# Prompt scores of the latent heads from multiplied-out keys: one product of 96 rows per score block in place of two

## What is computed

```python
kv = (c_kv @ w_ukv).reshape(B, T, A_HEADS, A_NOPE + A_VDIM)
k_nope, v = kv[..., :A_NOPE], kv[..., A_NOPE:]
s = (einsum('bqhd,bkhd->bhqk', qn, k_nope)          # prompt, 64 numbers per head
     + einsum('bqhr,bkr->bhqk', qr, k_r)) * scale   # 32 rotary numbers
...
q_lat = einsum('bqhd,chd->bqhc', q_nope, w_uk)      # samples: the query goes into the latent space
s_past = (einsum('bqhc,bkc->bhqk', q_lat, past_c)
          + einsum('bqhr,bkr->bhqk', q_rope, past_r)) * scale
```

## Time and profile before

| what | value |
|---|---|
| median of 3 runs | 2074.73 us (2072.35 to 2075.08) |
| the profiled execution | span 2076.9 us from its first to its last instruction; no other time of it is on record |
| PE busy | 2055.7 us, 99% of the span |
| DVE, ACT, POOL busy | 1530.8, 1284.6, 119.9 us |
| latent score steps of layer 0 / layer 1 | from 91.7 us / from 1121.2 us of the span |

### The profile page before, as it was taken

The page is one execution under the profiler, slowest core; times in us unless marked ns, Lnnn a source line. Parts: engine busy times, 40 slices in busy tenths (PEclk is TensorE's granted clock), DMA queues, the critical chain, the costliest instruction groups (busy, mean ns, idle before and its releaser), DMA issues.

```text
span 2076.9 us, 40622 instructions
## 1 busy us (share of the span) xinstructions
PE 2055.7 (99%) x15546; PEld 1794.8 (86%) x15546; DVE 1530.8 (74%) x3491; ACT 1284.6 (62%) x2535; POOL 119.9 (6%) x138
## 2 busy tenths in 40 slices
PE   8999999999999999999999999999999999999998
PEld 6776799999999888788887758999999998887887
DVE  5844589868899776576678436998688997766766
ACT  5464445658888665565564544556688886555654
POOL 2200010000000010100022000100000001101000
PEclk9999999999999999999999999999999999999999
DMA  9443437776666888898763543577766668888886
GB/s 313 154 150 143 163 126 254 248 253 221 216 215 214 286 304 296 303 319 279 253 226 141 170 170 116 180 253 250 246 221 209 220 214 300 311 290 295 266 269 220
DMA packets 137376, 481.76 MB, mean 232 GB/s; under 512 B 25666, under 2 KB 42082, under 8 KB 130768
## 3 DMA queue, kind: packets, MB, share of 16 engines
q1 hardware_dynamic: 124640, 438.45, 62.6%
q0 software_dynamic: 10496, 40.42, 5.6%
q10 hardware_dynamic: 2048, 0.30, 0.1%
HBM read 475.83 MB, written 104.21 MB: 279 GB/s over the span
## 4 chain that ended last, share of the span: by engine, by line
PE 98%; DVE 1%; ACT 1%; DMA 0%; issue 0%; DVEq 0%; ACTq 0%
PE ps L1194 35%; PE ps L1241 33%; PE ps L827 4%; PE ps L875 4%; PE ps L919 3%; PE ps L1206 3%; PE ps L1157 2%; PE ps L927 2%; PE ps L1165 1%; PE ps L1161 1%; PE ps L884 1%; PE ps L1016 1%; PE ps L1180 1%; PE ps L1019 1%; PE ps L978 1%; PE ps L1032 1%
## 5 line engine op out<-in xcount | busy, mean ns | idle before, releaser
L2165 DVE TENSOR_TENSOR parts<-region,parts 128x1024 fp32r<-128x1024 f32 x512 | 625.6, 1222 | 300.6 <-ACT parts L1509 298.0
L1194 PE MATMUL ps<-tokens_hi,parts 128*128 128x256 f32 x4096 | 760.5, 284 | 0.0
L1509 ACT CAST parts<-region 128x1024 fp32r<-128x1024 f32 x512 | 538.8, 1052 | 271.0 <-PE ps L1241 221.2
L1241 PE MATMUL ps<-parts,parts_hw 128*128 128x512 f32 x3024 | 688.7, 389 | 0.0
L1241 PEld LDWEIGHTS ps<-parts,parts_hw 128*128 128x128 f32 x3024 | 566.8, 188 | 124.0 <-DVE parts_hw L2215 6.9
L1194 PEld LDWEIGHTS ps<-tokens_hi,parts 128*128 128x128 f32 x4096 | 636.6, 188 | 1.0 <-issue 0.8
L1194 PE MATMUL ps<-parts_hw,parts 128*128 128x256 f32 x2048 | 573.7, 280 | 0.0
L1194 PEld LDWEIGHTS ps<-parts_hw,parts 128*128 128x128 f32 x2048 | 386.5, 189 | 0.0
L1555 ACT ACTIVATE big<-ps 128x256 f32<-128x256 f32 (+31 forms) x252 | 131.7, 523 | 146.9 <-PE ps L1194 146.8
L1543 ACT CAST parts_hw<-big 128x256 fp32r<-128x256 f32 x256 | 170.9, 668 | 0.7 <-DVE big L2226 0.7
L1536 ACT ACTIVATE region<-region 128x128 f16<-128x128 f16 x512 | 169.2, 436 | 0.0
(11 more groups left out here) (316 smaller groups left out, 2172.9 us busy)
## 6 DMA issues: line engine op xcount, KB each, us to landing
region<-in_peer_uT SPq DMA_DIRECT2D x256, 512.0 KB, 4.1
region<-in_peer_v SPq DMA_DIRECT2D x256, 512.0 KB, 4.7
out<-in_state_win_k SPq DMA_DIRECT2D x112, 384.0 KB
out<-in_state_win_v SPq DMA_DIRECT2D x112, 384.0 KB
big<-in_window_keysT SPq DMA_DIRECT2D x16, 576.0 KB, 3.8
big<-in_state_win_v SPq DMA_DIRECT2D x48, 192.0 KB, 4.2
region<-in_w_out SPq DMA_DIRECT2D x4, 2048.0 KB, 8.2
big<-in_peer_wq SPq DMA_DIRECT2D x4, 2048.0 KB, 13.7
```

Source lines behind the costliest of these rows:

```text
L1194: mm = pe.matmul(ps[:, j % ZB, 0:SEQ], a, hp[b][:, c, :], start=(c == 0 and n == 0), stop=(c == KD - 1 and n == 2))
L1241: mm = pe.matmul(ps[:, 2 * half + t, :], w_t[a][:, 128 * t:128 * t + 128], v_t[b][:, 512 * half:512 * half + 512], start=(j == 0 and n == ...
L1509: act.copy(hi_t[n % HIGHS], rows_t[n % ROWS]).then_inc(high[l], 1)
L2165: dve.tensor_tensor(lo_t[n % ROWS], rows_t[n % ROWS], hi_t[n % HIGHS], ALU.subtract).then_inc(low[l], 1)
```

## The change

The keys of the prompt are multiplied out once per layer. Three new products `kn` (`wuk` by the latents, two heads each, 256 columns) give the 64 key numbers of each head; DVE copies them to `khT`, rows 0 to 63, one head per copy, and before that writes the rotary keys of all six heads to rows 64 to 95 with one copy (32 partitions by 1536). The queries `qhT` are transposed head by head, 96 rows (64 and the rotary 32) at once, six jobs in place of the five of `qnT` and `qrT`. The score job is then one matmul per block, over 96 rows. The product into the latent space is left for the 8 sample tokens alone (`ql`, six matmuls of 8 columns into one bank). `kn` and `va` move ahead of `qbT` and `kbT`. `wuk` is a new load of 192 KB; `ukT` is laid out with 64 rows of 3072 bytes in place of 128 of 1536. ACT copies each half of `q` at once.

```diff
 jobs += [(("q", t, n), "A") for t in range(3) for n in range(2)]
+jobs += [(("kn", g), "V") for g in range(HP)]
+jobs += [(("va", t), "A") for t in range(2)]
 jobs += [(("qbT", g), "V") ...] + [(("kbT", g), "V") ...]
-jobs += [(("qnT", g), "A") for g in range(HP)] + [(("qrT", g), "A") for g in range(2)] + [(("qrS",), "A")]
-jobs += [(("qlT", h), "V") for h in range(NH)]
-jobs += [(("va", t), "A") for t in range(2)]
+jobs += [(("qhT", h), "A") for h in range(NH)] + [(("qrS",), "A")]
+jobs += [(("ql",), "V")]
...
 # SP
-sp.dma_start(wuv..., wukv_src[:, 1]).then_inc(uq_ld, 16)
+for a, dst in enumerate((wuk, wuv)):
+    sp.dma_start(dst..., wukv_src[:, a]).then_inc(uq_ld, 16)
...
 # PE
+wait_moved(pe, "ckvT")
+for g in range(HP):
+    dense(("kn", g), [(wuk[:, 128 * g:128 * g + 128], ckvT[:, 0:SEQ])], 128, SEQ)
+for t in range(2):
+    dense(("va", t), [(ckvT[:, 128 * t:128 * t + 128], wuv)], 128, 384)
...
-for g in range(HP):
-    turn("qnT", g, parts=tokens(q, 128 * g))
 pe.wait_ge(q_ready, 1)
-for g, hs in enumerate((4, 2)):
-    turn("qrT", g, parts=tokens(q, NH * NOPE + 128 * g, 32 * hs))
+for h in range(NH):
+    turn("qhT", h, parts=tokens(q, UQ // NH * h, NOPE + ROPE))
 turn("qrS", ...)
-wait_moved(pe, "qnT", HP - 1)
+wait_moved(pe, "qhT", NH - 1)
+o = begin("ql")
 for h in range(NH):
-    dense(("qlT", h), [(ukT[r0:r0 + 64, h // 2, :], qnT[r0:r0 + 64, h // 2, :])], 128, T)
-for t in range(2):
-    dense(("va", t), ...)
-wait_moved(pe, "qlT", NH - 1)
+    mm = pe.matmul(o[:, NB * h:NB * h + NB], ukT[:, h, :], qhT[0:NOPE, h, SEQ:T], start=True, stop=True)
+mm.then_inc(product[now[0]], 1)
+wait_moved(pe, "kn", HP - 1)
...
-pe.matmul(o[:, c0:c0 + K], qlT[:, h, qs], ckvT[:, 0:K], start=True, stop=False)
-mm = pe.matmul(o[:, c0:c0 + K], qrT[r0:r0 + 32, h // 4, qs], krT[r0:r0 + 32, 0:K], start=False, stop=True)
+mm = pe.matmul(o[:, c0:c0 + K], qhT[:, h, qs], khT[:, h, 0:K], start=True, stop=True)
...
 # DVE, behind the copy that announces q_ready
+wait_moved(dve, "krT")
+step(dve.tensor_copy(khT[NOPE:NOPE + ROPE], krT[NOPE:NOPE + ROPE, 0:SEQ].unsqueeze(1).to_broadcast([ROPE, NH, SEQ])))
+for g in range(HP):          # head_keys(g)
+    o = read("kn", g)
+    step(dve.tensor_copy(khT[0:NOPE, 2 * g, :], o[0:NOPE, 0:SEQ]))
+    settle()
+    dve.tensor_copy(khT[0:NOPE, 2 * g + 1, :], o[NOPE:128, 0:SEQ]).then_inc(moved_v[now[0]], 1)
 # qbT and kbT copies, taps
-for h in range(NH):
-    o = read("qlT", h)
-    dve.tensor_copy(qlT[:, h, :], o[:, 0:T]).then_inc(moved_v[now[0]], 1)
 step(dve.memset(qlS, 0.0))
-dve.tensor_copy(qlS[:, :, 0:NH], qlT[:, :, SEQ:T]...).then_inc(spread_set, 1)
+o = read("ql")
+dve.tensor_copy(qlS[:, :, 0:NH], o[:, 0:48]...).then_inc(moved_v[now[0]], 1)
```

More of the change, by code:

```diff
@@ L275, in program @@
         W_AT = at[0]
[L276 to L279, removed]
+        dead = big[:, at[0]:at[0] + NB * LAT]
+        ukT = cut(NH * LAT)[0:NOPE].rearrange("p (h c) -> p h c", h=NH)
+        qhT = cut(NH * T)[0:NOPE + ROPE].rearrange("p (h t) -> p h t", h=NH)
+        khT = cut(NH * SEQ)[0:NOPE + ROPE].rearrange("p (h t) -> p h t", h=NH)
         qkT = cut(2 * HP * T)
@@ L1394, in _ @@
                         o = read("q", t, n)
-                        oh = o[0:m, 0:288].rearrange("p (h x) -> p h x", h=3)
-                        qn = q[0:m, t, 192 * n:192 * n + 192].rearrange("p (h x) -> p h x", h=3)
-                        qr = q[0:m, t, NH * NOPE + 96 * n:NH * NOPE + 96 * n + 96].rearrange("p (h x) -> p h x", h=3)
-                        act.copy(qn, oh[:, :, 0:NOPE])
-                        act.copy(qr, oh[:, :, NOPE:]).then_inc(moved_a[now[0]], 1)
-                for g in range(HP):
-                    o = read("qnT", g)
-                    act.copy(qnT[:, g, :], o[:, 0:T]).then_inc(moved_a[now[0]], 1)
-                o = read("qrT", 0)
-                act.copy(qrT[:, 0, :], o[:, 0:T]).then_inc(moved_a[now[0]], 1)
-                o = read("qrT", 1)
-                act.copy(qrT[0:64, 1, :], o[0:64, 0:T]).then_inc(moved_a[now[0]], 1)
+                        act.copy(q[0:m, t, 288 * n:288 * n + 288], o[0:m, 0:288]).then_inc(moved_a[now[0]], 1)
+                for t in range(2):
+                    o = read("va", t)
+                    act.copy(va[:, t, :], o[:, 0:384]).then_inc(moved_a[now[0]], 1)
+                for h in range(NH):
+                    o = read("qhT", h)
+                    act.copy(qhT[:, h, :], o[0:NOPE + ROPE, 0:T]).then_inc(moved_a[now[0]], 1)
                 o = read("qrS")
@@ L1410, in _ @@
                 e.then_inc(moved_a[now[0]], 1)
-                for t in range(2):
-                    o = read("va", t)
-                    act.copy(va[:, t, :], o[:, 0:384]).then_inc(moved_a[now[0]], 1)
                 for s in range(2 * NH + 2):
@@ L1803, in _ @@
                 settle()
-                dve.tensor_copy(qrr[0:NB], q[0:NB, 2, NH * NOPE:].rearrange("p (h c) -> p h c", h=NH).unsqueeze(2).to_broadcast([NB, NH, 4, ROPE])).then_inc(q_ready, 1)
+                dve.tensor_copy(qrr[0:NB], q[0:NB, 2, :].rearrange("p (h c) -> p h c", h=NH)[:, :, NOPE:].unsqueeze(2).to_broadcast([NB, NH, 4, ROPE])).then_inc(q_ready, 1)
+                wait_moved(dve, "krT")
+                step(dve.tensor_copy(khT[NOPE:NOPE + ROPE], krT[NOPE:NOPE + ROPE, 0:SEQ].unsqueeze(1).to_broadcast([ROPE, NH, SEQ])))
+                for g in range(HP):
+                    head_keys(g)
                 for g in range(HP):
@@ L1811, in _ @@
                 some_taps(TAPS_AHEAD[4])
-                for h in range(NH):
-                    o = read("qlT", h)
-                    dve.tensor_copy(qlT[:, h, :], o[:, 0:T]).then_inc(moved_v[now[0]], 1)
-                settle()
-                dve.wait_ge(moved_v[now[0]], READ["qlT", NH - 1][1])
                 dve.wait_ge(product[now[0]], NUM["qrS",] + 1)
@@ L1819, in _ @@
                 settle()
-                dve.tensor_copy(qlS[:, :, 0:NH], qlT[:, :, SEQ:T].rearrange("p h b -> p b h")).then_inc(spread_set, 1)
+                o = read("ql")
+                dve.tensor_copy(qlS[:, :, 0:NH], o[:, 0:48].rearrange("p (h b) -> p b h", h=NH)).then_inc(moved_v[now[0]], 1)
                 def past_max(b):
```

27 lines of the change are left out of this document (11 added, 16 removed).

## The result

| | before | after |
|---|---|---|
| median | 2072.15 us (2066.55 to 2075.08, 8 runs) | 2078.93 us (2074.85 to 2082.25, 8 runs) |
| ratio, 95% interval | | 1.0031 [1.0019, 1.0043] |
| span of the profiled execution | 2076.9 us | 2080.4 us |
| PE at 0.50 in it, without the last 6 us | 17.1 us | 44.4 us |

A forecast was written before the change was run, and what follows sets the result against it. PE, busy 99% of the span, was the bound. Per layer: scores -7.7, added work +1.8, waits +0.4, given back +2.4, sum -3.1 us; -6.2 for two layers from 2074.7 gave 2068.5 us, range 2064.0 to 2073.0.

The forecast's parts named there:

- Query products, `kn` and `va`: PE ahead of the scores: `kn` adds 1.4 us per layer; `va`, priced at 1.36 us, only moves.
- 42 transpositions: PE ahead of the scores: 42 transpositions in place of 39, +0.5 us per layer.
- `ql`: Product for the sample tokens ahead of the scores: 1.5 us against `qlT`'s 1.57, so nothing gained or lost.
- Score job: Latent head's scores on PE: 0.76 us instead of 2.09, saving 7.7 us per layer for six heads.
- Given back: Score steps 1 to 4: PE held back by ACT loses 1.2, 1.2, 0.8 and 0.1 us again, rounded sum 2.4 per layer.
- A pair of copies of `kn`: DVE's copies, 0.73 us per pair, hold the banks of `kbT`; PE waits some 0.2 to 0.3 us.
- the `ukT` layout: Load of `ukT` in another layout with the same bytes: costed at nothing; PE had waited 0.46 us for it.
- even or equal: Rule that DVE copies within SBUF run at double speed if both sides' outermost dimensions are so; wide copy priced 0.9 us.
- rivals 1 and 2: Scores stay at 1.05 us per head, 2069.6 us, chance 0.12; DVE's wide copy runs slow, 2070.1 us, chance 0.12.
- rival 5: TensorE's clock falls ahead of the score steps, 12 us low per layer, making the kernel slower: 2080.5 us; chance 0.06.
- The one row against the fall, 85 to 90 at 1.00: Argument against the clock falling: from 85 to 90 us, nearly all transpositions and half-array work, it stayed 1.00.
- PHASE: Rival in the experiments' expectations, not the prediction: clock falls come and go whatever the order of work; no chance given.

The follow-up runs named there:

- e3: Changed kernel with DVE's wide copy of the rotary keys moved ahead of the rotation of q, PE's order untouched; 2070.46 us, ratio 1.0.
- the second execution of before: The kernel before, unchanged, profiled once more; 2066.74 us, span 2064.9.
- e9: Kernel before with its latent product cut to 8 columns per head, `va` kept in place and no wait added; 2073.4 us, ratio 1.0001.
- e7: Kernel before with seven small DVE copies ahead of the copies of `qbT` and `kbT`, so PE waits among its transpositions; 2079.41 us, ratio 1.0031.
- e10: Changed kernel with wide copy ahead of q's rotation, `ukT` awaited only ahead of `ql`, `kn` and `va` spread at three places between transpositions; 2066.7 us, ratio 0.9977.
- e4: Changed kernel with `ukT`'s load on its own semaphore, awaited ahead of `ql` instead of the query products; 2078.68 us, ratio 1.0034.
- e5: Changed kernel with `kn` and `va` behind `kbT`, wide copy behind the copies of `kbT`, `ukT` awaited only ahead of `ql`; 2071.6 us, ratio 0.9993.
- e8: Changed kernel plus sixteen unread filler matmuls of 256 columns, two passes each, ahead of `ql`; 2091.05 us.
- e2: Changed kernel with `kn` and `va` moved behind `kbT`, DVE's wide and head copies behind its `qbT` and `kbT` copies; 2073.01 us, ratio 1.0011.
- e6: Changed kernel with wide copy ahead of q's rotation, `kn` and `va` together behind `kbT`, `ukT` awaited only ahead of `ql`; 2069.04 us, ratio 0.9991.
- e1: Changed kernel plus one dense filler matmul of 256 columns ahead of each of the nine `kbT` and `qhT` jobs per layer; 2081.44 us.

## Why the prediction was wrong

**The sum was right, for full clock.** It said nothing of how long the clock would hold. Its parts by the rows of e3, layer 0:
- Query products, `kn` and `va`: 8.80 for 34 passes against 6.12 for 24, +2.7; forecast 1.4 + 1.36. 42 transpositions: 6.65, +0.6; forecast +0.5. `ql` 1.43; forecast 1.5.
- Score job: 0.76 at 92.50 and 0.66 at 95.45. In the changed kernel, at full clock: 0.66, 0.83, 0.69, 0.85, 0.76 for heads 1 to 5; mean 0.76, as forecast.
- Given back, by the distance that the 20 transpositions of a step take, 2.24 before (93.83 to 96.07): 2.69 in step 1 of e3 (96.11 to 98.80), 3.28 in step 2 of the changed kernel (108.34 to 111.62) and 0.2 more at `SC` 1, 3.12 in step 3 (116.24 to 119.36). So 0.45, 1.25 and 0.9, forecast 0.3, 1.2 and 0.8 (the changed kernel itself has 0.3 in step 1). The idle times in the brackets are smaller (0.34, 0.67 + 0.16, 0.47): part of the holding back is in the pace.
- The block: 55.53 against 59.00, -3.5. The forecast, without the waits that e3 takes out, was -7.7 + 1.8 + 2.4 = -3.5.

**Two small terms were short.** A pair of copies of `kn` comes each 0.90 us (85.24 to 86.14), not 0.73: so 0.63 us of waits in place of 0.2 to 0.3 (the prediction's own times of banks and jobs add up to 0.4). And the `ukT` layout, costed at nothing, was not nothing: PE waited 1.20 and 1.09 us in place of 0.46 and 0.42. From issue to landing the load took 3.1 and 3.0 us, against 2.3 in the second execution of before, and in both traces the DMA engines had nothing to do for over 2 us ahead of it, so `wuk`'s load wasn't in its way. That it is the smaller number of longer rows I read from these traces alone; the load wasn't tried in the old layout.

**Two readings were loose, and nothing hangs on them.** L1748 goes over 3 token groups on both sides, so by the prediction's words "even or equal" it would be fast too, yet its 384 elements took the 0.55 of L1804's 768; only L1804 and the new copy (0.95 for 1536) fit them. And two thirds of rivals 1 and 2 are 0.16, not 0.14.

**The step that failed is the clock, taken as given.** The sum has no term for it, and rival 5, which has, was put at 0.06. Measured were 30.7 us at 0.50 in the two blocks, where the sum had none. Rival 5 had the mechanism, its place, its length (12 us at 0.50 per layer; measured 13.7, and 3.4 more in layer 1) and nearly its time (2080.5; measured 2078.9). That the two times lie so close is in part luck: rival 5 adds 5.8 us to 2074.7 and leaves the waits at 0.4 per layer; measured were 6.8 on 2072.15, with 0.6 to 0.8 of waits for DVE and 0.7 more for `ukT` in each layer.

The one row against the fall, 85 to 90 at 1.00, was read as "transpositions are harmless". But in that row the stretch is flanked by the query products (to 82.74) and by `qlT` and `va` (from 88.81). The second of these is what the change takes away: `qlT` is cut to 8 columns and `va` moves ahead. e9 shows that with the first of its two parts cut the clock can fall there, in one layer of two. The other half was in the forecast too: waits of 0.2 to 0.3 us, costed at their own length. e7 shows one of 0.55 costing 3.7.

The Trainium skill, "TensorE: Matmul & The Clock Gate", Part 4, which says that transpositions don't count as a busy PE in the same way for this gate, was set aside on account of the earlier trace rows. e9 and e10 agree with it: like transpositions lose the clock (e9, layer 0, 10.2 us) or keep it (e10, both layers) by what dense work is put around them.

**The cause is a sum of two.** In all ten blocks with a wait of 0.3 us or more inside the transpositions (the changed kernel, e4, e5, e7, e8) the clock fell. In those without such a wait and without dense work in between (e3, e9) it fell in two of four; with dense work in the middle (e2, e6) in one of four at that place, for 3.4 us; with fillers among them (e1) in both, for 3.4 us each, behind the last filler; with dense work at three places (e10) or behind the transpositions (before, twice) in none of six. These are one or two traces of a kernel; the mean clocks of all executions have the same order (below 0.995: 8 of 8 and 8 of 8 for the changed kernel and e4, 6 of 10 for e3, 3 of 12 for e10, 0 of 76 before). PHASE as the whole account is out by them. What exactly the gate looks at, these runs don't tell. Nor is it settled why the fall behind the attention comes in one execution of the kernel before and not in the next; a difference of 3.1 to 4.6 us there runs through all medians, so the blocks are the better measure.

## What to carry to other kernels

Before taking dense matmuls away from between transpositions, or putting a wait among them, ask what keeps TensorE's clock up there: here 0.6 us of waiting cost 6 us of one block (61.82 against 55.53; 8.5 us in the medians, for both layers), and a change with which the kernel can be 7 us shorter made it 7 us longer. The work that is there anyway is the cheapest guard: spread dense products between the transpositions and let the producer's copies run early, rather than add fillers. And a stretch at full clock shows only that it holds with its neighbours as they are.

## What the runs showed of the hardware

- A wait of 0.55 us of TensorE among transpositions went with 6.8 us at 1.2 GHz from its end or 1.35 us behind it, even with 16 dense passes behind the transpositions (e7, both layers).
- The same kernel before has a mean granted clock of 0.999 to 0.995 from execution to execution, and times of 2066.3 to 2075.8 us in that order (76 executions).
- 10.24 us at 0.50 cost 4.6 us, 0.45 per microsecond.
- Two executions of the same kernel differ by 12 us of span (2076.9 and 2064.9), 7.7 of it in whether the clock falls behind the attention of either layer.
- A score job of two blocks over 96 rows took 0.66 to 0.85 us, mean 0.76, which is the price forecast from rows over 128. The same blocks over 128 rows took 1.05 between pieces over 32 rows. Whether the change of row count makes the difference, no run separates.
- A copy from 32 partitions by 1536, one source read six times, took 0.95 us, where 768 elements took 0.55; a copy of 64 partitions by 256 columns from PSUM took 0.42 to 0.43, and the next, which waits for it, began 0.45 after its start.
